# Moving the remainders of two weight units per chunk of the second layer from VectorE to GpSimd

## The reference, cut to what matters

```
for i in range(2):
    h = rms_norm(x, attn_norm[i])
    x = x + (fox_mixer if i == 0 else swa_mixer)(h, ...)
    h = rms_norm(x, ffn_norm[i])
    x = x + conv_glu_ffn(h, w_up[i], conv_w[i], conv_b[i], w_down[i])
```

## Time and profile before

| | |
|---|---|
| median of three runs | 2106.72 us |
| the profiled execution's own time | 2106.78 us |
| its span in the trace | 2105.0 us |
| TensorE busy | 2094.9 us |
| VectorE busy | 1285.8 us |
| ScalarE busy | 1008.8 us |
| GpSimd busy | 0.7 us |
| mean granted TensorE clock | 1.00 |

### The profile page before, as it was taken

One profiled execution on the slowest core, in us unless ns is written; L12 is line 12 of the kernel. 1 busy time (PEld: TensorE's weight loads), 2 busy tenths in 40 slices (PEclk: granted clock), 3 DMA queues, 4 the chain that ended last, 5 costly groups with the idle time before them and its releaser, 6 DMA issues.

```text
span 2105.0 us, 30259 instructions
## 1 busy us (share of the span) xinstructions
PE 2094.9 (100%) x10938; PEld 1791.4 (85%) x10938; DVE 1285.8 (61%) x1529; ACT 1008.8 (48%) x1321; POOL 0.7 (0%) x5
## 2 busy tenths in 40 slices
PE   9999999999999999999999999999999999999999
PEld 8888888888888888888888877888888888888887
DVE  5664565566676677654445676566676676664443
ACT  6554554544444444444444566554444444443333
POOL 0000000000000000000000000000000000000000
PEclk9999999999999999999999999999999999999999
DMA  7665555655655565566666544565565565566665
GB/s 249 210 180 170 165 175 172 188 175 185 192 193 184 189 199 176 188 208 192 189 191 191 179 139 139 177 187 171 197 196 174 189 199 193 177 205 193 191 196 162
DMA packets 206265, 390.69 MB, mean 186 GB/s; under 512 B 12860, under 2 KB 17772, under 8 KB 206188
## 3 DMA queue, kind: packets, MB, share of 16 engines
q1 hardware_dynamic: 203884, 387.45, 58.8%
q10 hardware_dynamic: 2304, 2.20, 0.3%
HBM read 387.48 MB, written 2.11 MB: 185 GB/s over the span
## 4 chain that ended last, share of the span: by engine, by line
PE 97%; DVE 2%; ACT 0%; issue 0%; DVEq 0%; ACTq 0%
PE ps L1126 47%; PE ps L1116 31%; PE ps L1122 16%; PE ps L1222 1%; DVE wlo L833 0%; PE ps L1274 0%; PE ps L1285 0%; PE ps L1302 0%; DVE qw L963 0%; PE ps L1319 0%; PE ps L1293 0%; PE ps L1336 0%; PE ps L1394 0%; DVE t L981 0%; PE ps L1264 0%
## 5 line engine op out<-in xcount | busy, mean ns | idle before, releaser
L833 DVE TENSOR_TENSOR wlo<-raw,whi 128x1024 fp32r<-128x1024 f32 x376 | 458.0, 1224 | 434.5 <-ACT whi L565 433.8
L1116 PE MATMUL ps<-hs,whi 128*128 128x512 f32 x2832 | 663.6, 390 | 0.0
L565 ACT ACTIVATE whi<-raw 128x1024 fp32r<-128x1024 f32 x378 | 399.8, 1060 | 499.9 <-PE ps L1126 484.4
L1116 PEld LDWEIGHTS ps<-hs,whi 128*128 128x128 f32 x2832 | 524.6, 188 | 104.3
L840 DVE TENSOR_TENSOR wlo<-raw,whi 128x1024 fp32r<-128x1024 f32 x352 | 414.6, 1221 | 288.1 <-PE ps L1122 256.0
L572 ACT ACTIVATE whi<-raw 128x1024 fp32r<-128x1024 f32 x352 | 365.9, 1056 | 263.0 <-DMA raw<-in_ffn_w_up 199.1
L1122 PEld LDWEIGHTS ps<-hs,wlo 128*128 128x128 f32 x2816 | 352.6, 191 | 8.7
L1122 PE MATMUL ps<-hs,wlo 128*128 128x256 f32 x2816 | 355.3, 283 | 0.0
L1126 PE MATMUL ps<-whi,gs 128*128 128x512 f32 x1408 | 348.5, 389 | 0.0
L1126 PEld LDWEIGHTS ps<-whi,gs 128*128 128x128 f32 x1408 | 264.0, 188 | 54.5
L1126 PE MATMUL ps<-whi,hs 128*128 128x512 f32 x1088 | 276.3, 396 | 0.7 <-ACT whi L565 0.7
(11 more groups left out here) (144 smaller groups left out, 855.3 us busy)
## 6 DMA issues: line engine op xcount, KB each, us to landing
raw<-in_ffn_w_up SPq DMA_DIRECT2D x352, 512.0 KB, 4.5
raw<-in_ffn_w_down SPq DMA_DIRECT2D x176, 512.0 KB, 4.2
raw<-in_fox_w_in SPq DMA_DIRECT2D x98, 512.0 KB, 3.9
raw<-in_swa_w_in SPq DMA_DIRECT2D x40, 512.0 KB, 3.8
raw<-in_fox_w_out SPq DMA_DIRECT2D x32, 512.0 KB, 3.7
raw<-in_swa_w_out SPq DMA_DIRECT2D x32, 512.0 KB, 3.7
xk<-in_x SPq DMA_DIRECT2D x8, 256.0 KB, 5.9
out_x<-xk SPq DMA_DIRECT2D x8, 256.0 KB, 4.4
```

The lines of the kernel that those rows point to most:

```text
L565: act.activation(whi[slot][:, :], raw[slot][:, :], ACT.Copy).then_inc(hi_ready, 1)
L833: tt(wlo[slot][:, :], raw[slot][:, :], whi[slot][:, :].bitcast(F32), ALU.subtract).then_inc(lo_ready, 1)
L1116: return pe.matmul(ps[:, bank, :], whi[slot][:, c:c + P], moving.rearrange("p h t -> p (h t)"), start=first, stop=last)
```

## The change

GpSimd makes the remainders of eight units: 21 and 22, 29 and 30, 37 and 38, 45 and 46, counted from the layer's first (21 to 38 are input units, 45 and 46 the sixth and seventh output unit). It waits for the high part of each, subtracts, and raises a new semaphore `lo_pool`. VectorE leaves these units out. When it comes to the unit behind each pair (23, 31, 39, 47) it waits until GpSimd has finished both and raises `lo_ready` by two in its name, so that the count stays in the order of the units; then it converts its own unit as before. TensorE, ScalarE and SyncE are unchanged in text.

```diff
@@ -212,6 +212,7 @@
         lo_ready = sem("lo_ready")
+        lo_pool = sem("lo_pool")
         unit_done = sem("unit_done")
@@ -417,6 +418,8 @@
+
+        POOL_UNITS = [U_SWA + 8 * c + i + RAW for c in range(2, SWA_CHUNKS + 1) for i in (1, 2)]
@@ -816,6 +819,10 @@
             pool.wait_ge(unit_done, U_SWA)
             pool.memset(prs[:, :, 0:2, CHUNK:P], 0.0).then_inc(g_zero, 1)
+            for u in POOL_UNITS:
+                pool.wait_ge(hi_ready, u + 1)
+                pool.tensor_tensor(wlo[u % RAW][:, :], raw[u % RAW][:, :], whi[u % RAW][:, :].bitcast(F32),
+                                   ALU.subtract).then_inc(lo_pool, 1)
@@ -825,6 +832,11 @@
             def conv_lo(u):
 
                 slot = u % RAW
+                if u in POOL_UNITS:
+                    return
+                if u - 1 in POOL_UNITS:
+                    dve.wait_ge(lo_pool, POOL_UNITS.index(u - 1) + 1)
+                    dve.sem_inc(lo_ready, 2)
                 dve.wait_ge(hi_ready, u + 1)
```

## The result

The changed kernel takes 2127.82 us (median of five runs, 2126.51 to 2128.23) against 2106.75 us: ratio 1.0099, 95% interval 1.0088 to 1.0110, 1% slower. Forecast were 2119.8 us and a range up to 2126.0. The sign was right, and so was the mechanism that the forecast counted, that the two engines take turns. A second one, TensorE's clock, was counted at nothing, and the size was wrong: +21.1 us in place of +13.1.

The account below looks back on a forecast made before the run. TensorE was taken to bound the kernel, waiting 4.6 us for VectorE in four rounds. Removal gains 1.49 us, but turns at SBUF make +3.2 and 9.9 us, sum +13.1: 2119.8 us, range 2104.8 to 2126.

Parts of the forecast that it names:

- TensorE's clock behind the stalls: TensorE after idling 3.5 to 4 us: a lower clock would add a few us, put only in the range's top.
- the forecast's own case: GpSimd and VectorE take turns at SBUF in the four rounds, s = 1: +13.1 us, 2119.8 us, chance 0.48.
- D: Duration of one GpSimd subtraction of 128x1024: taken as 2.2 us, between 1.5 and 3.2 us moving the forecast 2114 to 2128.
- Turns for whole instructions: Upper bound for both engines reading SBUF: VectorE held for whole GpSimd instructions, +13.1 us in sum.
- s: Share of the turn-taking holding that is real: result -1.5 + 14.6 s us, forecast at s = 1.
- the mixed case at half speed: Both engines slow to half speed while together: +7.3 us, 2114.1 us; chance 0.22 shared with rival (b).
- The chain: VectorE's `wr1`, `wr2`, and `pn2` in rounds 2 to 4, four places where TensorE waits: +3.2 us, then +3.3 each.
- The removal: Eight VectorE conversions of 1.22 us go: 0.77 us gained in round 1, 0.24 us in each other, 1.49 in all.
- ScalarE's `ess` is late next: Rounds 2 to 4: the second `pn2` waits for ScalarE's last exponential, limiting the gain to 0.24 us each.
- The moved count and the waits: `lo_ready` raised later, delaying SyncE's loads with 5 us left, and VectorE's added wait and raise: cost 0.
- Rival (a): VectorE's port is its own, GpSimd does not hold it: -1.49 us, 2105.3 us, chance 0.22.
- Rival (b): Turns, but VectorE keeps its place while its queue is not empty: +9.1 us, 2115.9 us; chance 0.22 with the mixed case.

Follow-up runs that it names:

- e1_fill: Changed kernel with 12 extra TensorE matmuls of 512 columns in each of the four `wqt` waits: 2119.19 us, ratio 1.0058.
- e8_delay: Kernel before, without GpSimd, with e3_order's later conversions and extra VectorE products ahead of the rotation in the four rounds: 2130.24 us, ratio 1.0110.
- e10_delay_fill: e8_delay with 16 extra TensorE matmuls in each of the four stalls: 2121.53 us, ratio 1.0070.
- e2_write: Changed kernel, but GpSimd fills its eight units with zeros twice instead of subtracting, so it writes and does not read: 2105.13 us, ratio 0.9992.
- e9_copy: Changed kernel, but GpSimd copies the high part (one input read) instead of subtracting: 2110.62 us, ratio 1.0018.
- e3_order: Kernel before, without GpSimd: VectorE converts units 21, 29, 37, 45 later, directly ahead of the second of each pair: 2105.13 us, ratio 0.9992.
- e4_order_act: e3_order, and ScalarE makes the high part of units 29, 37, 45 one step later too: 2102.38 us, ratio 0.9978 against the kernel before.
- e6_second: Changed kernel with GpSimd making only the second unit of each pair (22, 30, 38, 46): 2121.55 us, ratio 1.0068.
- e7_behind: Changed kernel with GpSimd making only one unit per chunk, the third of the group's (23, 31, 39, 47): 2106.98 us, ratio 1.0000.
- e5_first: Changed kernel with GpSimd making only the first unit of each pair (21, 29, 37, 45): 2114.33 us, ratio 1.0035.

## Why the prediction was wrong in size, point by point

- **TensorE's clock behind the stalls: the step that failed.** The prediction said that if TensorE "came back at the lower of its clock levels, it would be a few us more", put that "in the top of the range" and counted nothing in the sum. It is 8.0 us by the trace, 8.6 by filling the idle time (e1_fill), 8.7 in a kernel without GpSimd (e8_delay less e10_delay_fill). The kernel before has a mean granted clock of 1.00, so nothing in it says whether 4 us of idle time bring it or how long it lasts. An estimate was possible all the same: if one unit of 2.72 us ran at half the rate behind each stall, that would be 2.7 us more, 11 us in four, and the range would have reached 2131. It belonged there, since the forecast's own case made the idle stretches of 4 us. The top of 2126 also lay below the 2128 us that the prediction itself worked out for D of 3.2 us, so in truth it had no room for the clock.
- **Turns for whole instructions.** Right, and s was 1: an instruction is held for all of what is left of the other. That also rules out the mixed case at half speed (s around 0.6). e2_write and e9_copy show that it is GpSimd's read, of one input or of two. The rule cited from the Trainium skill (SBUF — State Buffer, section "Who interferes with whom") agrees with this trace: blocked fully, 1.45 us for a sum of 0.16, and not beside GpSimd's fills.
- **The chain.** +3.2 us in round 1 as forecast to 0.1; +3.0 against +3.3 in the others. In all 12.2 against 13.1. That this is so near is in part luck. D was 2.44 us where nothing stood in its way, against 2.2, and by the prediction's own 0.8 us for each 0.1 us of D that alone would have given 15.0. On the other side, not all of D is holding: in round 1 VectorE's two products are held for 2.21 and 2.16 us, and in rounds 2 to 4 the second subtraction holds the product `prs` for 2.64 - 0.69 = 1.95 us only, since the reciprocal (0.2 us, one input) runs under it, and I had counted all of D.
- **The removal.** 0.77 + 3 x 0.24 = 1.5 us forecast, 1.7 to 1.8 us measured (e3_order, e2_write). That ScalarE's `ess` is late next was right: with it moved (e4_order_act) the three stalls of 1.05 us are gone but for 0.3 us in all.
- **The moved count and the waits.** They were forecast to cost nothing, and they cost nothing: e2_write has both.
- **Rival (a), no interference,** is refuted for a GpSimd instruction that reads and right for one that writes. **Rival (b),** VectorE keeping its place, is refuted in round 1 of the changed kernel: between the rows at 1187.55 and 1190.90 there is no gap, and GpSimd, whose row begins at 1190.17, got in between the two. Whether it always does is open: in e6_second GpSimd's row begins at 1190.23, and VectorE's product at 1190.48 still ran in 0.68 us before it was let in; in round 2 of the same kernel it got in between two products. No run was made to settle this.

## What to carry to other kernels

Before work is given to GpSimd, list what VectorE runs in the same microseconds: in this kernel every instruction there with two inputs in SBUF was held until the GpSimd instruction that reads SBUF was through, so the price is set by the place (0 in e7_behind, 2.2 us in e6_second for the same instruction) and not by how busy the engines are. Cost a stall of TensorE with the clock that may fall in it, here about 2 us on top of each stall of 4 us, and in some executions 1.6 us already behind one of 1.9 or 2.4 us. And look first for a conversion that can simply stand later in its own queue.

## What the runs showed of the hardware that was not expected

- A VectorE sum over four elements took 1.45 us, and a product of 128x512 2.85 us, while GpSimd subtracted; beside GpSimd's fills the same products took their 0.69 us.
- On GpSimd a subtraction of 128x1024 float32 takes 2.44 us, a copy 1.09 and a fill 0.95; the fill of half the size takes 0.53.
- A granted clock of 0.50 was seen behind a stall of TensorE of 4.0 us, 0.75 in the mean of 4 us behind one of 2.36 us (e5_first) and 0.78 behind one of 1.91 us (e9_copy). Behind the three other stalls of each of these two executions (1.84 to 2.36 and 1.19 to 1.92 us) it was 1.00, so the length of the stall alone does not decide it here. The kernels whose clock fell have a spread of 1.7 to 3.3 us between runs, those whose stalls were filled or short mostly 0.2 to 1.
